# A layer normalisation's variance by a product with a matrix of ones and a Newton step, inside one inference step of a convolution trunk

## Chip, cores and metric

One core of a Trainium2 chip. The time is that of the whole program on the device, in microseconds (us); three runs of each kernel are compared by their median.

## What is computed

The program is one layer of a streaming encoder on 4096 prompt frames and 32 frames of a running stream, 1024 channels, all in fp32. Cut to what matters:

```python
def mixer_layer(x, hist_a, hist_b, norm_g, w_in, conv_a_w, conv_b_w, conv_b_bias, ln_b_g, ln_b_b, w_out):
    hn = rms_norm(x, norm_g)
    proj = jnp.einsum('btd,de->bte', hn, w_in.astype(hn.dtype))
    h_a, b_a, c_a, z_a, a_b, g_b, z_b = jnp.split(proj, SPLITS, axis=-1)
    conv_a, new_a = causal_dwconv(hist_a, c_a * h_a, conv_a_w)
    out_a = b_a * conv_a * jax.nn.silu(z_a)
    v_b = a_b * jax.nn.sigmoid(g_b)
    conv_b, new_b = causal_dwconv(hist_b, v_b, conv_b_w)
    s_b = jax.nn.silu(layer_norm(conv_b + conv_b_bias, ln_b_g, ln_b_b))
    out_b = s_b * jax.nn.silu(z_b)
    mixed = jnp.concatenate([out_a, out_b], axis=-1)
    y = jnp.einsum('bte,ed->btd', mixed, w_out.astype(mixed.dtype))
    return x + y, new_a, new_b
```

A second `rms_norm` follows. The change is in `layer_norm`, which takes mean and variance of each frame over the 512 channels of group B, and in the order of the work around it.

## The kernel before

Channels lie on the partitions and frames along the free dimension, so the sums of the layer normalisation run across partitions, and TensorE makes them. Every large product is a Strassen product: seven products P1, P5, P6, P2, P7, P3, P4 (in this order) of half-sized blocks, each as split products (high and low parts in fp32r, three matmuls for each piece of 128 rows; lines 2422 to 2424).

The program has two large parts. The input projection and both convolutions run first (VectorE makes the 31 taps of convolution B; line 2149). The output part, which the change touches most, follows. It runs over 16 pairs of row tiles, m = 0 to 15, 256 frames each, and over the seven products i = 0 to 6 of a pair. The layer normalisation works on blocks L of 512 frames, two pairs to a block; the work for block L is spread over the 14 products (slots 0 to 13) of pairs m = 2(L-1) and 2L-1, one block ahead of the pairs that use it. The last block, L = 8, is 128 wide. Block 0 is normalised in the late part of the projection.

There is no scheduler. Each engine runs a list written by hand, and semaphores order them. Inside the loop over (m, i), a table `LN_SLOT` (and `FIRST_LN_SLOT` for block 1) says in which slot each step of the normalisation is issued on each engine, and inside one slot the order is that of the code.

What has to be known of these lists for the steps below:

- GpSimd makes the channel sums of the next block in slot 12 (`sums`, lines 1309 and 1312), behind the low part of the next pair's P1 form (`form_low`, line 1352). ScalarE makes the high part of the sum (`sum_high`, line 1672), GpSimd the low part (line 1317), TensorE the mean (`mean`, lines 2530 and 2531) behind product 0.
- VectorE subtracts the mean (`centre`, line 2161), ScalarE squares, VectorE adds the squares (`square_sums`, lines 2166 and 2168).
- TensorE then sums the squares by `column_sums` (slot 5), with the squares as the weights and one column of ones moving, 128 frames at a time, so that frames come to lie on partitions. ScalarE scales (line 1677), GpSimd takes the power -0.5 (line 1323), and `column_spread` (slot 7) spreads the result over all partitions with an identity.
- VectorE multiplies by it (`normalise`, line 2175, slot 7), ScalarE applies SiLU (line 1684, slot 8), VectorE multiplies by the gate (`gate`, line 2189, slot 10).
- VectorE adds each product from PSUM into the rows (`add_product`, line 2340). P6 uses the bank of P1, P7 that of P6, P4 that of P7 and P3 that of P5, so each of these products waits for the addition before it. VectorE also scales finished rows (`finish_rows`, line 2347) and makes the sums and low parts of the next pair's forms (lines 2205 to 2226) in slots 5 and 6 of a pair.
- ScalarE makes the high parts of the forms (`form_high_of`, line 1648): P1 at i = 4, P5 and P6 at i = 5, each in program order behind whatever stands ahead of it.

Of the kernel before, what the change touches and what calls it, by code (L numbers as in the profile page):

```python
# [4 lines left out]
F32 = mybir.dt.float32  # L5
# [5 lines left out]
P = 128  # L11
# [231 lines left out]
def build_program(nc, A):  # L243
    ctx = ExitStack()
    with ctx:
# [35 lines left out]
        var_cols = sb("ln_var_columns", [P, RT])  # L281
        rstd_cols = sb("ln_rstd_columns", [P, RT])
# [247 lines left out]
        ln_cols_sum = sem("ln_columns_summed")  # L530
        ln_cols_var = sem("ln_columns_var")
        ln_cols_rstd = sem("ln_columns_rstd")
# [150 lines left out]
        def col_tiles(L):  # L683
            return 1 if is_last(L) else RT
# [58 lines left out]
        def h_part_of(m, i):  # L743
# [3 lines left out]
        FIRST_LN_SLOT = {"sums": 1, "sum_high": 3, "sum_low": 3, "mean": 4, "squares": 5, "square_sums": 6, "columns": 8,  # L747
                         "spread": 10, "silus": 11, "gate": 12}
        LN_SLOT = {"sums": -2, "sum_high": -2, "sum_low": -2, "mean": 1, "squares": 2, "square_sums": 3, "columns": 5,
                   "spread": 7, "silus": 8, "gate": 10}  # L750
# [13 lines left out]
        def _(sp):  # L764
# [187 lines left out]
            def first_loads(g, c):  # L952
# [12 lines left out]
                if g == 11 and c in (0, 2):  # L965
                    if c == 0:
# [3 lines left out]
                        sp.wait_ge(ln, ln_event(0, "squares"))  # L970
                    else:
                        sp.wait_ge(ln_cols_sum, 1)
# [4 lines left out]
                if g == 13 and c == 0:  # L977
                    sp.wait_ge(dve_made, DVE_AT[period_of("bz", 4, JT - 1), "z"])
                    sp.wait_ge(u_state, 16 * 8)
                    load_x_rows(0)  # L980
# [165 lines left out]
        def _(pool):  # L1146
# [154 lines left out]
            def sums(L):  # L1301
# [5 lines left out]
                else:  # L1307
                    pool.wait_ge(ln, ln_event(L - 1, "gated" if L == 1 else "squares"))
# [106 lines left out]
            for n in range(III, PERIODS):  # L1415
# [8 lines left out]
                for part in range(3):  # L1424
                    for r in late_split(n, part):
                        late_low(r)
                    if part == 0 and g == 10:
                        column_rstd(0)
# [5 lines left out]
            for m in range(PAIRS):  # L1434
                for i in range(7):
# [6 lines left out]
                    if ln_due(m, i, "columns"):  # L1442
                        column_rstd(ln_due(m, i, "columns"))
# [19 lines left out]
        def _(act):  # L1463
# [210 lines left out]
            def column_var(L):  # L1674
                c = col_tiles(L)
                act.wait_ge(ln_cols_sum, L + 1)
# [117 lines left out]
            for n in range(III, PERIODS):  # L1794
# [11 lines left out]
                if g == 10:  # L1806
                    column_var(0)
# [893 lines left out]
```

## Time and profile before

| | |
|---|---|
| median of 3 runs | 1511.53 us (1511.13 to 1513.31) |
| profiled execution, its own time | 1511.45 us |
| its span | 1509.7 us |
| TensorE (PE) busy | 1500.2 us, 99% |
| weight loads (PEld) busy | 1323.4 us, 88% |
| VectorE (DVE) busy | 1307.6 us, 87% |
| ScalarE (ACT) busy | 594.4 us, 39% |
| GpSimd (POOL) busy | 653.5 us, 43% |
| granted TensorE clock | 0.999 |

Shares are of the span, averaged over the program. In the listings a start time is counted from the start of the span, and a group shows its count, its busy time and the mean of one.

### The profile page before, as it was taken

Reading aid. Unit: us, or ns where it says so; the run is one execution under the profiler, and the core shown is the slowest. Engines: PE = TensorE matmul, PEld = TensorE weight load, DVE = VectorE, ACT = ScalarE, POOL = GpSimd, SP = SyncE. Lnnn points to the kernel's source line nnn. Section 1 sums busy time; section 2 is a strip of 40 time slices with the busy share of each in tenths; the row PEclk is TensorE's granted clock in tenths of the full one; section 3 lists DMA queues with packets and bytes.
Section 4 is the critical chain, followed back from the end, with each engine's and each line's share of the span. In section 5 each row is a group of like instructions: output and inputs, shape, how many; then the busy total and the mean of one; then the engine's idle time right before and its main releaser. Section 6 shows DMA issues by size and latency. Waiting matters only on the chain.

```text
span 1509.7 us, 19729 instructions
## 1 busy us (share of the span) xinstructions
PE 1500.2 (99%) x7114; PEld 1323.4 (88%) x7114; DVE 1307.6 (87%) x1333; ACT 594.4 (39%) x987; POOL 653.5 (43%) x568
## 2 busy tenths in 40 slices
PE   9999999999999999999999999999999999999998
PEld 8999999888888888888888888888888878888886
DVE  7899999999998898899899895798898798888876
ACT  7554432432342343333253322224343344444433
POOL 4887778311424232332532252116664544444441
PEclk9999999999999999999999999999999999999999
DMA  6797968688988889999889888766877755455541
GB/s 250 306 352 289 366 254 321 211 301 310 317 287 294 281 279 336 303 342 283 262 271 320 311 269 261 242 214 213 237 223 227 265 193 170 172 189 186 177 153 70
DMA packets 119512, 388.97 MB, mean 258 GB/s; under 512 B 17848, under 2 KB 23096, under 8 KB 115832
## 3 DMA queue, kind: packets, MB, share of 16 engines
q1 hardware_dynamic: 116872, 387.57, 75.5%
q8 instruction: 57, 0.93, 0.2%
q10 hardware_dynamic: 2544, 0.14, 0.1%
q14 instruction: 39, 0.32, 0.1%
HBM read 279.19 MB, written 108.47 MB: 257 GB/s over the span
## 4 chain that ended last, share of the span: by engine, by line
PE 98%; DVE 2%; issue 0%; ACT 0%; POOL 0%; POOLq 0%; DVEq 0%; ACTq 0%
PE ps L2422 32%; PE ps L2424 32%; PE ps L2423 32%; PE ps L2544 0%; PE ps L2537 0%; PE ps L2557 0%; DVE conv_b L2189 0%; DVE h_rows_odd L2347 0%; DVE w_ring L2212 0%; DVE ln_tmp_b L2166 0%; DVE w_ring_f L2161 0%; PE ps L2628 0%; PE ps L2531 0%; PE ps L2530 0%; DVE ps L2205 0%
## 5 line engine op out<-in xcount | busy, mean ns | idle before, releaser
L2149 DVE SCALAR_TENSOR_TENSOR ps<-v,conv_b_taps,ps 128x920 f32<-128x920 f32 (+2 forms) x580 | 630.8, 1088 | 17.3
L2422 PE MATMUL ps<-xf,w_ring 128*128 128x460 f32 (+1 forms) x1624 | 602.9, 371 | 0.3 <-issue 0.3
L2424 PE MATMUL ps<-xf,w_ring 128*128 128x460 f32 (+1 forms) x1624 | 602.6, 371 | 0.0
L2423 PE MATMUL ps<-xf,w_ring 128*128 128x460 f32 (+1 forms) x1624 | 600.8, 370 | 0.0
L2422 PEld LDWEIGHTS ps<-xf,w_ring 128*128 128x128 f32 x1624 | 305.4, 188 | 34.2 <-issue 1.2
L2423 PEld LDWEIGHTS ps<-xf,w_ring 128*128 128x128 f32 x1624 | 305.4, 188 | 34.0
L2424 PEld LDWEIGHTS ps<-xf,w_ring 128*128 128x128 f32 x1624 | 304.9, 188 | 34.2
L1605 ACT ACTIVATE sets<-ps 128x460 f32<-128x460 f32 x168 | 92.8, 553 | 475.9 <-PE ps L2424 475.9
L1346 POOL TENSOR_TENSOR w_ring<-w_ring_f,w_ring 128x512 fp32r<-128x512 f32 x28 | 38.9, 1388 | 215.3 <-ACT w_ring L1635 215.3
L1297 POOL TENSOR_TENSOR sets<-sets 128x460 f32<-128x460 f32 x42 | 56.5, 1346 | 129.1 <-ACT sets L1605 129.1
L1237 POOL TENSOR_TENSOR w_ring<-w_ring_f,w_ring 128x512 fp32r<-128x512 f32 x56 | 74.9, 1349 | 64.4 <-ACT w_ring L1539 64.0
L2422 PE MATMUL ps<-out_forms,w_ring 128*128 128x512 f32 x240 | 94.5, 394 | 0.3 <-DVE h_rows_even L2340 0.3
L2424 PE MATMUL ps<-out_forms,w_ring 128*128 128x512 f32 x240 | 93.5, 390 | 0.0
L2423 PE MATMUL ps<-out_forms,w_ring 128*128 128x512 f32 x240 | 93.5, 389 | 0.0
L2422 PE MATMUL ps<-xf 128*128 128x448 f32 (+1 forms) x224 | 83.3, 372 | 0.0
L2424 PE MATMUL ps<-xf 128*128 128x448 f32 (+1 forms) x224 | 82.6, 369 | 0.0
L2423 PE MATMUL ps<-xf 128*128 128x448 f32 (+1 forms) x224 | 82.3, 367 | 0.0
L1196 POOL TENSOR_TENSOR x_raw<-x_raw,rstd_spread 128x460 f32<-128x460 f32 x56 | 68.0, 1249 | 32.2 <-DMA rstd_spread<-rstd_spill 32.2
L2340 DVE TENSOR_TENSOR h_rows_odd<-ps,h_rows_odd 128x512 f32<-128x512 f32 x56 | 38.5, 687 | 30.5 <-PE ps L2424 30.5
L1539 ACT ACTIVATE w_ring<-w_ring_f 128x512 fp32r<-128x512 f32 x56 | 35.0, 631 | 72.3 <-DMA w_ring_f<-in_w_in 72.1
L2422 PEld LDWEIGHTS ps<-out_forms,w_ring 128*128 128x128 f32 x240 | 45.1, 188 | 10.2 <-issue 0.7
L2424 PEld LDWEIGHTS ps<-out_forms,w_ring 128*128 128x128 f32 x240 | 45.0, 188 | 9.7
(237 smaller groups left out, 2216.9 us busy)
## 6 DMA issues: line engine op xcount, KB each, us to landing
w_ring<-weight_forms SPq DMA_DIRECT2D x294, 512.0 KB, 5.4
weight_forms<-xf SPq DMA_DIRECT2D x7, 2048.0 KB, 12.6
weight_forms<-w_ring SPq DMA_DIRECT2D x7, 2048.0 KB, 11.4
x_row<-in_x_prompt SPq DMA_DIRECT2D x28, 512.0 KB, 7.4
out_weight_forms<-w_ring SPq DMA_DIRECT2D x28, 512.0 KB, 6.6
w_ring_f<-in_w_in SPq DMA_DIRECT2D x56, 256.0 KB, 3.5
x_raw<-in_xT SPq DMA_DIRECT2D x31, 460.0 KB, 6.9
xf_f<-in_w_in SPq DMA_DIRECT2D x24, 512.0 KB, 6.3
```

Source lines behind the costliest of these rows:

```text
L1196: pool.tensor_tensor(part, part, spread[:, 0:TB], ALU.mult).then_inc(x_scaled, 1)
L1237: pool.tensor_tensor(ring[:, slot, 1, :], ring_f32[:, slot, 1, :], ring[:, slot, 0, :].bitcast(F32), ALU.subtract).then_inc(late_lo, 1)
L1297: pool.tensor_tensor(sets[:, s, QC, :], sets[:, s, QC, :], sets[:, s, QD, :], ALU.add).then_inc(c22_made, 1)
L1346: pool.tensor_tensor(low, of, high, ALU.subtract).then_inc(wr_lo, 1)
L1539: act.activation(ring[:, slot, 0, :], ring_f32[:, slot, 1, :], ACT.Copy).then_inc(late_hi, 1)
L1605: act.activation(sets[:, n % 2, quarter, :], ps[:, bank, 0:TB], ACT.Copy).then_inc(copied, 1)
L2149: dve.scalar_tensor_tensor(dst, window, wb[:, j, k:k + 1], part, ALU.mult, ALU.add).then_inc(taps_done, 1)
L2340: dve.tensor_tensor(to, ps[:, bank_of_product(m, i), :], to, ALU.add).then_inc(h_add, 1)
L2422: pe.matmul(out, ahi, bhi, start=(start and x == 0), stop=False, skip_group_check=goes_on)
L2423: pe.matmul(out, ahi, blo, start=False, stop=False, skip_group_check=goes_on)
L2424: mm = pe.matmul(out, alo, bhi, start=False, stop=(stop and x == len(terms) - 1), skip_group_check=goes_on)
```

## The change

The variance is now a product of the sum of squares with the same matrix `mean_w` that the mean uses (1/512 everywhere). For that the sum of squares is split into a high part (ScalarE) and a low part (VectorE). The result stands in PSUM on all partitions at once. ScalarE makes a first value of the inverse root as exp(-0.5 ln(var + eps)), and VectorE refines it with one Newton step of three operations. The two column products, the scaling on ScalarE and the power on GpSimd are gone.

The slots of the later steps change: normalise from 7 to 10, SiLU from 8 to 10, gate from 10 to 12. VectorE's list changes too: for even m, the additions of the previous pair's P4 and of P1 go into `last_lows_of(m)`, ahead of the low parts of P7 and P3; for odd m both row scalings stand in slot 1.

```diff
-        LN_SLOT = {"sums": -2, "sum_high": -2, "sum_low": -2, "mean": 1, "squares": 2, "square_sums": 3, "columns": 5,
-                   "spread": 7, "silus": 8, "gate": 10}
+        LN_SLOT = {"sums": -2, "sum_high": -2, "sum_low": -2, "mean": 1, "squares": 2, "square_sums": 3, "square_sum_parts": 4,
+                   "variance": 5, "seed": 7, "rstd": 9, "normalise": 10, "silus": 10, "gate": 12}
...
-            def column_rstd(L):
-                c = col_tiles(L)
-                pool.wait_ge(ln_cols_var, L + 1)
-                pool.tensor_tensor(rstd_cols[:, 0:c], var_cols[:, 0:c], minus_half[:, :].to_broadcast([P, c]),
-                                   ALU.pow).then_inc(ln_cols_rstd, 1)
...
+            def square_sum_high(L):
+
+                w = ln_width(L)
+                act.wait_ge(ln, ln_event(L, "squares"))
+                act.activation(ta_split[:, 1, 0:w], tb[:, 0, 0:w], ACT.Copy).then_inc(ln_var_hi, 1)
+
+            def rstd_seed(L):
+
+                w = ln_width(L)
+                act.wait_ge(ln_var, L + 1)
+                act.activation(ln_rstd_places(L)[0], ps[:, STAT_BANK, 0:w], ACT.Ln,
+                               bias=ln_eps[:, :]).then_inc(ln_log, 1)
+                act.wait_ge(ln_log, L + 1)
+                act.activation(ln_rstd_places(L)[0], ln_rstd_places(L)[0], ACT.Exp, scale=-0.5).then_inc(ln_seed, 1)
...
+            def square_sum_low(L):
+
+                w = ln_width(L)
+                dve.wait_ge(ln_var_hi, L + 1)
+                dve.tensor_tensor(ta_split[:, 0, 0:w], tb[:, 0, 0:w], ta_split[:, 1, 0:w].bitcast(F32),
+                                  ALU.subtract).then_inc(ln_var_lo, 1)
+
+            def refine_rstd(L):
+
+                w, (y, t) = ln_width(L), ln_rstd_places(L)
+                dve.wait_ge(ln_seed, L + 1)
+                dve.scalar_tensor_tensor(t, y, -0.5, y, ALU.mult, ALU.mult).then_inc(ln_step, 1)
+                dve.wait_ge(ln_step, 3 * L + 1)
+                dve.scalar_tensor_tensor(t, ps[:, STAT_BANK, 0:w], ln_eps[:, :], t, ALU.add, ALU.mult).then_inc(ln_step, 1)
+                dve.wait_ge(ln_step, 3 * L + 2)
+                dve.scalar_tensor_tensor(y, t, 1.5, y, ALU.add, ALU.mult).then_inc(ln_step, 1)
...
@@ last_lows_of
-                if m == 2:
-                    add_product(1, P4)
-                    add_product(2, P1)
+                if m and m % 2 == 0:
+                    add_product(m - 1, P4)
+                    add_product(m, P1)
                 low_of(m, P7, 0)
                 low_of(m, P3, 1)
...
@@ VectorE's loop over (m, i)
-                    elif m and m != 2 and i in (1, 2):
+                    if m % 2 and i == 1:
+                        finish_rows(m - 1, 0)
+                        finish_rows(m - 1, 1)
+                    elif m % 2 == 0 and m > 2 and i in (1, 2):
                         finish_rows(m - 1, i - 1)
...
@@ TensorE
-            def column_sums(L):
-            def column_spread(L):
+            def variance(L):
+
+                w, dst = ln_width(L), ps[:, STAT_BANK, :]
+                pe.wait_ge(ln_var_lo, L + 1)
+                pe.matmul(dst[:, 0:w], mean_w[:, :], ta_split[:, 1, 0:w], start=True, stop=False)
+                pe.matmul(dst[:, 0:w], mean_w[:, :], ta_split[:, 0, 0:w], start=False, stop=True).then_inc(ln_var, 1)
```

**VectorE, an odd pair of the steady output part.** The first list is of before, from the row scaling and addition behind P4 of the even pair to the sums for the next pair; h_rows are the output rows, the 2048-wide operations are normalise (line 2175) and gate (line 2189).

```order
L2340 TENSOR_TENSOR h_rows_even<-ps,h_rows_even 128x512
L2175 TENSOR_TENSOR conv_b<-conv_b,ps 128x2048
L2340 TENSOR_TENSOR h_rows_odd<-ps,h_rows_odd 128x512
L2347 SCALAR_TENSOR_TENSOR h_rows_even<-h_rows_even,rstd,final_gain 128x1024
L2340 TENSOR_TENSOR h_rows_odd<-ps,h_rows_odd 128x512
L2347 SCALAR_TENSOR_TENSOR h_rows_even<-h_rows_even,rstd,final_gain 128x1024
L2340 TENSOR_TENSOR h_rows_odd<-ps,h_rows_odd 128x512
L2189 TENSOR_TENSOR conv_b<-conv_b,silu_zb 128x2048
L2340 TENSOR_TENSOR h_rows_odd<-ps,h_rows_odd 128x512 x2
L2205 TENSOR_TENSOR ps<-out_a,conv_b 128x512
```

Now the same stretch of the changed kernel, whose lines have other numbers (2367 is the addition, 2374 the row scaling, 2189 to 2193 the Newton step, 2200 normalise, 2214 gate).

```order
L2367 TENSOR_TENSOR h_rows_even<-ps,h_rows_even 128x512
L2367 TENSOR_TENSOR h_rows_odd<-ps,h_rows_odd 128x512
L2374 SCALAR_TENSOR_TENSOR h_rows_even<-h_rows_even,rstd,final_gain 128x1024 x2
L2367 TENSOR_TENSOR h_rows_odd<-ps,h_rows_odd 128x512
L2189 SCALAR_TENSOR_TENSOR ln_tmp_b<-ln_tmp_b 128x512
L2191 SCALAR_TENSOR_TENSOR ln_tmp_b<-ps,ln_eps,ln_tmp_b 128x512
L2193 SCALAR_TENSOR_TENSOR ln_tmp_b<-ln_tmp_b 128x512
L2367 TENSOR_TENSOR h_rows_odd<-ps,h_rows_odd 128x512
L2200 TENSOR_TENSOR conv_b<-conv_b,ln_tmp_b 128x2048
L2367 TENSOR_TENSOR h_rows_odd<-ps,h_rows_odd 128x512 x2
L2214 TENSOR_TENSOR conv_b<-conv_b,silu_zb 128x2048
```

Normalise has moved behind the additions of P1, P5 and P6 of the odd pair, both row scalings and the Newton step, and the gate now stands directly ahead of the sums for the next pair.

**ScalarE, the same place.** In the changed kernel 1679 and 1682 are the logarithm and the exponential, 1688 SiLU, 1643 a form's high part (`<-out_a` is P1's of the next pair, `<-ps` P5's and P6's) and 1667 the high part of the next block's channel sum.

```order
L1679 ACT_TABLE_LOAD
L1679 ACTIVATE ln_tmp_b<-ps,ln_eps 128x512
L1682 ACT_TABLE_LOAD
L1682 ACTIVATE ln_tmp_b<-ln_tmp_b 128x512
L1688 ACT_TABLE_LOAD
L1688 ACTIVATE conv_b<-conv_b,ln_b,ln_g 128x512 x4
L1643 ACTIVATE out_in_form<-out_a 128x512
L1667 ACTIVATE w_ring<-w_ring_f 128x512
L1643 ACTIVATE w_ring<-ps 128x512 x2
```

Before, this stretch begins with SiLU and is the same from there on; what is new are three table loads and two activations ahead of it, and that SiLU itself waits for the later normalise.

## Rows read from the trace of the kernel before

**Rows 1.** The page's busy times, and the chain that ended last

```profile
PE 1500.2 (99%) x7114; PEld 1323.4 (88%) x7114; DVE 1307.6 (87%) x1333; ACT 594.4 (39%) x987; POOL 653.5 (43%) x568
...
PE 98%; DVE 2%; issue 0%; ACT 0%; POOL 0%; POOLq 0%; DVEq 0%; ACTq 0%
```

**Rows 2.** Group by line and form: the column sums (busy, mean ns)

```profile
L2537 PE MATMUL ps<-ones,ln_tmp_b 128*128 128x1 f32 x66 | 8.0, 240 | 1.4 <-DVE ln_tmp_b L2168 1.4
```

**Rows 3.** Timeline of TensorE around mean and column products (start, duration)

```profile
1295.72 0.39 PE L2530 MATMUL ps<-w_ring,mean_w 128*128 128x512 f32 x1
...
1296.18 0.40 PE L2422 MATMUL ps<-out_forms,w_ring 128*128 128x512 f32 x1
...
1307.09 0.95 PE L2537 MATMUL ps<-ones,ln_tmp_b 128*128 128x1 f32 x8
...
1308.22 0.40 PE L2423 MATMUL ps<-out_form_p,w_ring 128*128 128x512 f32 x1
...
1313.56 1.05 PE L2544 MATMUL ps<-ident,ln_rstd_columns 128*128 128x128 f32 x8
...
1314.69 0.39 PE L2423 MATMUL ps<-out_forms,w_ring 128*128 128x512 f32 x1
```

**Rows 4.** The critical chain: two column sums one block apart

```profile
1266.59 0.79 PE ps L2537 x8
...
1307.25 0.79 PE ps L2537 x8
```

**Rows 5.** Timeline of VectorE, pairs 5 to 7 (a bracket gives idle time before)

```profile
1290.73 0.69 DVE L2212 TENSOR_TENSOR w_ring<-ps,w_ring 128x512 fp32r<-128x512 f32 x1 [0.72 <-ACT w_ring L1648]
...
1293.86 0.68 DVE L2212 TENSOR_TENSOR out_in_form<-ps,out_in_form 128x512 fp32r<-128x512 f32 x1
...
1295.92 0.69 DVE L2340 TENSOR_TENSOR h_rows_even<-ps,h_rows_even 128x512 f32<-128x512 f32 x1
1296.53 2.28 DVE L2161 TENSOR_TENSOR w_ring_f<-w_ring_f,ps 128x2048 f32<-128x2048 f32 x1
1298.72 1.42 DVE L2347 SCALAR_TENSOR_TENSOR h_rows_odd<-h_rows_odd,rstd,final_gain 128x1024 f32<-128x1024 f32 x1
...
1301.86 0.68 DVE L2340 TENSOR_TENSOR h_rows_even<-ps,h_rows_even 128x512 f32<-128x512 f32 x1
...
1304.20 0.69 DVE L2168 TENSOR_TENSOR ln_tmp_b<-ln_tmp_b 128x512 f32<-128x512 f32 x1
...
1307.29 0.69 DVE L2340 TENSOR_TENSOR h_rows_even<-ps,h_rows_even 128x512 f32<-128x512 f32 x1 [1.79 <-PE ps L2424]
...
1314.60 0.68 DVE L2340 TENSOR_TENSOR h_rows_even<-ps,h_rows_even 128x512 f32<-128x512 f32 x1
```

**Rows 6.** Timeline of ScalarE: SiLU and a form's high part, pair 5

```profile
1276.85 2.94 ACT L1684 ACTIVATE conv_b<-conv_b,ln_b,ln_g 128x512 f32<-128x512 f32 x4 [1.47 <-DVE conv_b L2175]
1279.69 0.62 ACT L1648 ACTIVATE w_ring<-out_a 128x512 fp32r<-128x512 f32 x1
```

**Rows 7.** Timeline of GpSimd: P1's low part, then the next block's sums

```profile
1280.38 2.13 POOL L1352 TENSOR_TENSOR w_ring<-out_a,w_ring 128x512 fp32r<-128x512 f32 x1 [2.69 <-ACT w_ring L1648]
1284.27 3.08 POOL L1309 TENSOR_TENSOR w_ring_f<-w_ring_f 128x1024 f32<-128x1024 f32 x1 [1.75 <-DMA w_ring_f<-conv_spill]
1287.43 1.29 POOL L1312 TENSOR_TENSOR w_ring_f<-w_ring_f 128x512 f32<-128x512 f32 x1
```

**Rows 8.** Timeline, end of pair 1: VectorE's gate, GpSimd's sums beside it

```profile
1204.34 4.24 DVE L2189 TENSOR_TENSOR conv_b<-conv_b,silu_zb 128x2048 f32<-128x2048 f32 x1
...
1204.03 2.40 POOL L1309 TENSOR_TENSOR w_ring_f<-w_ring_f 128x1024 f32<-128x1024 f32 x1 [4.47 <-DMA w_ring_f<-conv_spill]
1206.51 3.23 POOL L1312 TENSOR_TENSOR w_ring_f<-w_ring_f 128x512 f32<-128x512 f32 x1
```

**Rows 9.** Timeline of ScalarE in the projection: a table load and the activation behind it

```profile
1122.25 1.28 ACT L1589 ACT_TABLE_LOAD   x1
1123.54 0.56 ACT L1589 ACTIVATE sets<-ps 128x460 f32<-128x460 f32 x1
```

More of the change, by code:

```diff
@@ L745, in h_part_of @@
             return hrow[m % 2][:, row, DA * half:DA * (half + 1)]
-        FIRST_LN_SLOT = {"sums": 1, "sum_high": 3, "sum_low": 3, "mean": 4, "squares": 5, "square_sums": 6, "columns": 8,
-                         "spread": 10, "silus": 11, "gate": 12}
-        LN_SLOT = {"sums": -2, "sum_high": -2, "sum_low": -2, "mean": 1, "squares": 2, "square_sums": 3, "columns": 5,
-                   "spread": 7, "silus": 8, "gate": 10}
+        FIRST_LN_SLOT = {"sums": 1, "sum_high": 3, "sum_low": 3, "mean": 4, "squares": 5, "square_sums": 6,
+                         "square_sum_parts": 6, "variance": 8, "seed": 8, "rstd": 9,
+                         "normalise": 10, "silus": 10, "gate": 12}
+        LN_SLOT = {"sums": -2, "sum_high": -2, "sum_low": -2, "mean": 1, "squares": 2, "square_sums": 3, "square_sum_parts": 4,
+                   "variance": 5, "seed": 7, "rstd": 9, "normalise": 10, "silus": 10, "gate": 12}
         def ln_due(m, i, step):
@@ L2324, in _ @@
                     first_ln[n - III](0)
+                if n - III == 11:
+                    normalise(0)
                 if n - III == 12:
@@ L2380, in _ @@
                 for i in range(7):
-                    if i and (m, i) not in ((0, 1), (1, 6), (2, 1)):
+                    if i and (m, i) != (1, 6) and (m % 2 or i > 1):
                         add_product(m, i - 1)
-                    elif m and i == 0 and m != 2:
+                    elif m % 2 and i == 0:
                         add_product(m - 1, P4)
@@ L2402, in _ @@
                         square_sums(ln_due(m, i, "square_sums"))
+                    if m == 2 and i == 3:
+                        finish_rows(1, 0)
+                        finish_rows(1, 1)
+                    if ln_due(m, i, "square_sum_parts"):
+                        square_sum_low(ln_due(m, i, "square_sum_parts"))
                     if m + 1 < PAIRS and i == 6:
@@ L2531, in mean @@
                 pe.matmul(dst[:, 0:w], mean_w[:, :], ta_split[:, 0, 0:w], start=False, stop=True).then_inc(ln_mean, 1)
-            def column_sums(L):
-                pe.wait_ge(ln, ln_event(L, "squares"))
-                for c in range(col_tiles(L)):
-                    mm = pe.matmul(ps[:, STAT_BANK, c:c + 1], tb[:, 0, P * c:P * (c + 1)], ones[:, :],
-                                   start=True, stop=True)
-                mm.then_inc(ln_cols_sum, 1)
-            def column_spread(L):
-                pe.wait_ge(ln_cols_rstd, L + 1)
-                for c in range(col_tiles(L)):
-                    mm = pe.matmul(ps[:, STAT_BANK, P * c:P * (c + 1)], rstd_cols[:, c:c + 1].to_broadcast([P, P]),
-                                   ident[:, :], start=True, stop=True)
-                mm.then_inc(ln_var, 1)
+            def variance(L):
[3 more added lines that the diff above has]
+                pe.matmul(dst[:, 0:w], mean_w[:, :], ta_split[:, 0, 0:w], start=False, stop=True).then_inc(ln_var, 1)
             def first_mean_square(b):
@@ L2584, in _ @@
                     mean(0)
[L2585 to L2586 removed]
                 if n == III + 11:
[L2588 removed]
+                    variance(0)
                 late_tile(n, 0)
@@ L2639, in _ @@
                         mean(ln_due(m, i, "mean"))
-                    if ln_due(m, i, "columns"):
-                        column_sums(ln_due(m, i, "columns"))
-                    if ln_due(m, i, "spread"):
-                        column_spread(ln_due(m, i, "spread"))
+                    if ln_due(m, i, "variance"):
+                        variance(ln_due(m, i, "variance"))
                     out_product(m, i)
```

64 lines of the change are left out of this document (29 added, 35 removed).

## Prediction, made before the result was known

> **What bounds the kernel now.** I read the busy times first: TensorE is busy 99% of the span, VectorE 87%, the other two about 40% [rows 1]. The chain that ended last says the same, 98% of it is TensorE. So two things can move the time: work taken off TensorE, microsecond for microsecond, and waits put into it, where nothing is hidden. VectorE's 13% idle looks like cover, but it is an average; what counts is in which slot a result is needed. So I went to the timelines of one block of the output part, two pairs, which repeats every 40.66 us (1266.59 to 1307.25) [rows 4].
>
> **What TensorE is spared.** Column sums: from the start of the eight matmuls to the second matmul of the next product 1.13 us pass (1307.09 to 1308.22) where one step of 0.23 would, so the group costs 0.90; the spread costs the same (1313.56 to 1314.69) [rows 3]. Together 1.80 us a block. The new variance is the pair of matmuls that the mean is: 1295.72 to 1296.18, 0.46 us [rows 3]. So 1.34 us less for each of the eight full blocks, and for the last, narrow one (2 of the 66 records of a kind [rows 2]) an estimated 0.3: 11.0 us in all. TensorE alone would need 40.66 - 1.34 = 39.3 us a block, and one slot of it is (1307.09 - 1296.18)/4 = 2.73 us [rows 3].
>
> **What the other engines get.** For each full block VectorE gets one 512-wide subtraction (0.69) and three 512-wide operations of the Newton step; I price them at 0.73 with their hand-over, from the 512-wide rows of 0.69 (a 1024-wide operation of their kind took 1.42) [rows 5]. Bounds: 0.61, the step between two additions, and 0.73. That is 2.9 us. ScalarE gets a copy of 0.62, two activations of about that size and three table loads; a load took 1.28 and the activation behind it began 0.01 after its end (1122.25, 1123.54) [rows 9]. GpSimd loses one small power. As totals all this fits. The loads stand ahead of their waits in ScalarE's list, so SiLU's is hidden while ScalarE waits for normalise.
>
> **The walk through one block.** What decides is the order. Normalise, SiLU and gate move from slots 7, 8, 10 to 10, 10, 12, and behind SiLU in ScalarE's list stand the high part of the next pair's P1 form, then the high part of the next block's channel sum, then those of P5 and P6. GpSimd makes P1's low part and only then the channel sums. So a late SiLU holds a chain over ScalarE, GpSimd, ScalarE and VectorE. I follow it from the start of P1's addition in an even pair (time 0), with durations of before:
>
> - VectorE, even pair: addition and the two low parts 3 x 0.61, centre to row scaling 2.19, scaling to P6's addition 3.14 (1298.72 to 1301.86) [rows 5]: that addition starts at 7.2. Then it and the 1024-wide sum of squares: before 2.34 to the next start (1301.86 to 1304.20), with GpSimd's low part of P1 beside it, which now comes later; I take 0.6 + 1.2, the 1.2 being half of the 2048-wide 2.28. The second sum (0.69) ends at 9.7, ScalarE's copy at 10.4, VectorE's low part at 11.2. TensorE's variance starts at 11.3 with its weight load.
> - TensorE: 0.46 + 3 x 2.73 and 0.2 of pipeline: P1 of the odd pair is done at 20.1. VectorE is there before: P7's to P4's addition took 7.3 (1307.29 to 1314.60) [rows 5], from 11.1 to 18.4.
> - VectorE, odd pair: P1's addition to 20.7, both scalings 2.5 (3.14 less an addition) to 23.3, P5's addition to 23.9, Newton step to 26.1, P6's addition to 26.7, normalise 2.28 to 29.0. The first value for the step is ready at about 23.7 (half row square 1.5 after P4's addition, two loads, two activations): just in time.
> - ScalarE: SiLU, then 2.84 after its start P1's high part (1276.85 to 1279.69) [rows 6], at 31.8. GpSimd starts P1's low part 0.69 later (1280.38), takes 2.13, then 3.16 and 1.29 for the sums [rows 7]: 39.1. ScalarE's two high parts 1.2: 40.4.
> - VectorE: low part of P5 to that of P7 3.13 (1290.73 to 1293.86), one more addition 0.6 [rows 5], then P1's addition of the next even pair: 44.2.
>
> This is a closed loop of 44.2 us, over three engines that each wait for another, longer than TensorE's own 39.3. Before, the same loop did not close, as SiLU stood two slots earlier: the sums began at 1284.27, after a wait for a DMA, and P1's addition came in time at 1295.92 [rows 5, 7]. So each block costs 44.2 - 40.7 = 3.5 us more, with TensorE waiting 4.9 in it: for the mean, for P6's addition ahead of P7, and for the low part of the squares ahead of the variance.
>
> **The sum.** Six passages from a block to the next (blocks 1 to 7): 6 x 3.5 = 21. In block 2 the row scalings stand between the second sum of squares and its low part: 0.5. In the late projection (block 0) 1.3 is spared, but VectorE gets 2.9 us more there; I take 0. The last block gives 0.3 back. 1511.45 + 21 + 0.5 - 0.3 = 1532.7, say 1533 us. The profiled execution's own time, 1511.45, is that of the median, 1511.53, so nothing is shifted.
>
> **Bounds.** GpSimd's three operations are what I know least: 2.13 + 3.16 + 1.29 = 6.6. Alone a 512-wide one took 1.29 and the 1024-wide as little as 2.40 [rows 7, 8]: 1.6 less, with the Newton step at 0.61 2.0 less, times six: 1521. Beside the gate, the second one took 3.23 [rows 8]: 1.9 more, 1545. In this spot the changed kernel's gate runs beside them in every block. The Trainium skill, GPSIMD Engine Reference, Specifications, says that GpSimd's SBUF interface is shared with VectorE and contended by VectorE instructions with two SBUF inputs; the gate is one. By that rule, the trace agrees: the gate took 4.24 us beside them, where centre, of the same width, took 2.28 [rows 5, 8].
>
> **Rivals.**
> - *Faster (the other side).* The loop is shorter than I make it, so TensorE waits for nothing and all 11.0 us come out: 1500.5. It decides at a loop of 40.66; for that 3.5 us of my walk would have to be wrong in one place, GpSimd's three operations taking 3.1 and not 6.6. For it: VectorE's idle share is larger than what it gets. Against it: even at the lower bounds the loop is 42.2. Chance 0.09, and 0.04 for a draw near 1511.
> - *Slower, but with GpSimd at its low rows:* 1521 to 1526, chance 0.17.
> - *The likeliest:* loop of 43.3 to 45.3 us, 1526 to 1540, chance 0.48.
> - *Contention in every block,* up to 1547: chance 0.14.
> - *The first value is late.* If a switch of tables cost more than its load, the Newton step would wait. At 1.4 us more for each of two switches it starts 2.6 later than in my walk; seven times, 18 on top: 1551. The row of before speaks against it: the activation began 0.01 after the load [rows 9]. Chance 0.05. The same end is reached if one of TensorE's waits grows so long that the granted clock falls to 1.2 GHz; before it was 0.999 throughout, with waits up to 1.4 us [rows 2]. Chance 0.03. The Trainium skill, ScalarE: Activation LUTs, What ACT_TABLE_LOAD costs, is the page that says so: 1.28 us for the load and 1.38 for a drain, 2.66 for each switch; by it the time would be that of this rival.
>
> **How the numbers follow.** A measurement of this kernel tells 0.2% (3 us) from no change. Faster 0.09, same 0.04, slower 0.87. From 1518 to 1547 the range leaves out the faster case and most of the last rival, under 2 in 10.
>
> **What would show it.** Right: no columns' matmuls; TensorE idle about 4 to 5 us in each block from pair 2 on, with VectorE's addition (P6's) and its low part of the squares as the ones it waits for, and GpSimd's mean part; the even pairs' P1 additions some 44 us apart; ScalarE's P5 high part started by the high part of the channel sum behind GpSimd. Wrong: additions 39.3 to 40 us apart and TensorE without idle time, or ScalarE's exponential as the releaser of the Newton step. What would break the prediction is GpSimd's part of the loop, or a transfer (the next block's convolution rows, which came at 1284.27 before) that starts later and takes its place.

## The result, and the profile after

The changed kernel takes 1553.35 us (median; 1551.37 to 1556.71), the kernel before 1511.87 us in the same runs. The ratio is 1.0273, with an interval of 1.0263 to 1.0284: slower by 41.5 us. The forecast was 1533, range 1518 to 1547: the direction is right, the time lies 6 us above the range, and the loss is twice the 21.5 that I gave it. The profiled execution took 1552.25 us, span 1550.5.

The page's busy times of the changed kernel, against [rows 1]:

```profile
PE 1510.5 (97%) x7000; PEld 1320.6 (85%) x7000; DVE 1330.5 (86%) x1369; ACT 640.8 (41%) x1031; POOL 643.4 (41%) x559
```

TensorE has 114 matmuls fewer and is busy 10 us more: part of its work ran slower. What it waited for (total us, times, longest), which was 1.4 us for the column sums before [rows 2]:

```profile
PE ps L2564 <- POOL w_ring L1322: 18.8, 6, 3.2
PE ps L2456 <- DVE h_rows_odd L2367: 9.0, 7, 2.4
...
PE ps L2571 <- DVE w_ring L2182: 1.8, 2, 1.4
```

L2564 is the mean's matmul, L1322 GpSimd's low part of the channel sum. P1's additions in the even pairs, VectorE's timeline, give the length of each block; first the changed kernel:

```profile
1172.89 0.68 DVE L2367 TENSOR_TENSOR h_rows_even<-ps,h_rows_even 128x512 f32<-128x512 f32 x1
...
1221.28 0.68 DVE L2367 TENSOR_TENSOR h_rows_even<-ps,h_rows_even 128x512 f32<-128x512 f32 x1
...
1361.30 0.68 DVE L2367 TENSOR_TENSOR h_rows_even<-ps,h_rows_even 128x512 f32<-128x512 f32 x1
...
1408.70 0.68 DVE L2367 TENSOR_TENSOR h_rows_even<-ps,h_rows_even 128x512 f32<-128x512 f32 x1
...
1454.71 0.68 DVE L2367 TENSOR_TENSOR h_rows_even<-ps,h_rows_even 128x512 f32<-128x512 f32 x1
...
1498.87 0.68 DVE L2367 TENSOR_TENSOR h_rows_even<-ps,h_rows_even 128x512 f32<-128x512 f32 x1
```

Then the first two and the last of the kernel before:

```profile
1171.58 0.68 DVE L2340 TENSOR_TENSOR h_rows_even<-ps,h_rows_even 128x512 f32<-128x512 f32 x1
...
1215.01 0.68 DVE L2340 TENSOR_TENSOR h_rows_even<-ps,h_rows_even 128x512 f32<-128x512 f32 x1
...
1458.56 0.69 DVE L2340 TENSOR_TENSOR h_rows_even<-ps,h_rows_even 128x512 f32<-128x512 f32 x1 [0.28 <-PE ps L2424]
```

When the output part starts the changed kernel is 1.3 us late; one block later 6.3; at its seventh addition 36.8 (1454.71, and 1458.56 less one block of 40.66); at the eighth 40.3. So the loss grows with every passage, by 3.5 to 6.7 us, and there are seven passages.

One passage closely, with time 0 at 1267.76, as in the walk of the prediction. VectorE:

```profile
1267.76 0.68 DVE L2367 TENSOR_TENSOR h_rows_even<-ps,h_rows_even 128x512 f32<-128x512 f32 x1
...
1288.57 0.69 DVE L2367 TENSOR_TENSOR h_rows_odd<-ps,h_rows_odd 128x512 f32<-128x512 f32 x1 [0.79 <-PE ps L2458]
1289.62 3.51 DVE L2374 SCALAR_TENSOR_TENSOR h_rows_even<-h_rows_even,rstd,final_gain 128x1024 f32<-128x1024 f32 x2 [0.36 <-POOL rstd L1169]
...
1293.65 0.68 DVE L2189 SCALAR_TENSOR_TENSOR ln_tmp_b<-ln_tmp_b 128x512 f32<-128x512 f32 x1
...
1296.36 2.28 DVE L2200 TENSOR_TENSOR conv_b<-conv_b,ln_tmp_b 128x2048 f32<-128x2048 f32 x1
...
1310.48 0.69 DVE L2237 TENSOR_TENSOR w_ring<-ps,w_ring 128x512 fp32r<-128x512 f32 x1 [4.03 <-ACT w_ring L1643]
...
1314.21 0.68 DVE L2367 TENSOR_TENSOR h_rows_even<-ps,h_rows_even 128x512 f32<-128x512 f32 x1
```

ScalarE: the first value of the inverse root, SiLU, P1's high part, the channel sum's:

```profile
1288.56 1.28 ACT L1679 ACT_TABLE_LOAD   x1
1289.86 0.69 ACT L1679 ACTIVATE ln_tmp_b<-ps,ln_eps 128x512 f32<-128x512 f32 x1
1290.56 1.28 ACT L1682 ACT_TABLE_LOAD   x1
1291.86 0.63 ACT L1682 ACTIVATE ln_tmp_b<-ln_tmp_b 128x512 f32<-128x512 f32 x1
...
1298.68 2.93 ACT L1688 ACTIVATE conv_b<-conv_b,ln_b,ln_g 128x512 f32<-128x512 f32 x4 [4.89 <-DVE conv_b L2200]
1301.52 0.62 ACT L1643 ACTIVATE w_ring<-out_a 128x512 fp32r<-128x512 f32 x1
1309.34 0.63 ACT L1667 ACTIVATE w_ring<-w_ring_f 128x512 fp32r<-128x512 f32 x1 [7.20 <-POOL w_ring_f L1317]
```

GpSimd: P4's low part, P1's, the two channel sums, the sum's low part:

```profile
1289.56 1.30 POOL L1351 TENSOR_TENSOR w_ring<-w_ring_f,w_ring 128x512 fp32r<-128x512 f32 x1
1302.21 2.95 POOL L1351 TENSOR_TENSOR w_ring<-out_a,w_ring 128x512 fp32r<-128x512 f32 x1 [11.36 <-ACT w_ring L1643]
1305.13 2.84 POOL L1314 TENSOR_TENSOR w_ring_f<-w_ring_f 128x1024 f32<-128x1024 f32 x1
1308.05 1.26 POOL L1317 TENSOR_TENSOR w_ring_f<-w_ring_f 128x512 f32<-128x512 f32 x1
1310.04 1.27 POOL L1322 TENSOR_TENSOR w_ring<-w_ring_f,w_ring 128x512 fp32r<-128x512 f32 x1 [0.74 <-ACT w_ring L1667]
```

This is the forecast's loop, station by station, and 46.45 us long where I had 44.2: P1's high part starts at 33.8 (mine 31.8), GpSimd's sums end at 41.6 (39.1), the next addition is at 46.45 (44.2). VectorE waits 4.03 and ScalarE 7.20 for GpSimd, TensorE 3.15 for the mean:

```profile
1311.37 0.59 PE L2564 MATMUL ps<-w_ring,mean_w 128*128 128x512 f32 x1 [3.15 <-POOL w_ring L1322]
...
1313.24 0.76 PE L2456 MATMUL ps<-out_forms,w_ring 128*128 128x512 f32 x1 [0.86 <-DVE h_rows_odd L2367]
1313.81 0.63 PE L2457 MATMUL ps<-out_forms,w_ring 128*128 128x512 f32 x1
1314.23 0.63 PE L2458 MATMUL ps<-out_forms,w_ring 128*128 128x512 f32 x1
```

The second wait ends with the addition at 1312.42, which stands behind VectorE's low parts. Behind the first wait the matmuls step by 0.42 us, not 0.23 (1313.81 to 1314.23). The stretches of the trace (columns: length, busy time and count of PE, PEld, DVE, ACT, POOL, the granted clock, then share and GB/s of the DMA engines) say why: 0.50 is the lower level, 1.2 GHz. The stretch from 1268 lies behind the wait for the mean one block earlier.

```profile
1240.00:1260.00 20.00, 20.00 (x88) 16.27 (x88) 16.72 (x16) 10.51 (x16) 6.42 (x6) 1.00 0.65 214
1268.00:1270.00 2.00, 2.00 (x6) 1.52 (x6) 2.00 (x4) 1.79 (x5) 0.04 (x1) 0.50 0.00 0
1300.00:1311.00 11.00, 8.12 (x35) 6.00 (x33) 5.41 (x5) 3.80 (x8) 7.97 (x4) 1.00 0.61 191
1312.00:1316.00 4.00, 3.14 (x8) 2.21 (x8) 4.00 (x7) 3.48 (x9) 1.43 (x2) 0.50 0.00 0
```

### The profile page after: what moved, and what is told of

Its sections match the earlier page's. It is cut to its first block and busy times, and to the rows that moved or that the text cites. A ratio compares the mean times of both kernels' runs of the same rounds, so it can differ in the third digit from the quotient of the medians.

```text
span 1550.5 us, 19572 instructions
## 1 busy us (share of the span) xinstructions
PE 1510.5 (97%) x7000; PEld 1320.6 (85%) x7000; DVE 1330.5 (86%) x1369; ACT 640.8 (41%) x1031; POOL 643.4 (41%) x559
## 5 line engine op out<-in xcount | busy, mean ns | idle before, releaser
L2456 PE MATMUL ps<-out_forms,w_ring 128*128 128x512 f32 x240 | 99.4, 414 | 9.8 <-DVE h_rows_odd L2367 7.7
L2457 PE MATMUL ps<-out_forms,w_ring 128*128 128x512 f32 x240 | 97.5, 406 | 0.0
L2458 PE MATMUL ps<-out_forms,w_ring 128*128 128x512 f32 x240 | 97.0, 404 | 0.0
L2456 PEld LDWEIGHTS ps<-out_forms,w_ring 128*128 128x128 f32 x240 | 47.4, 197 | 25.8 <-DVE w_ring L2237 9.1
L1351 POOL TENSOR_TENSOR w_ring<-out_a,w_ring 128x512 fp32r<-128x512 f32 x11 | 22.6, 2052 | 88.6 <-ACT w_ring L1643 88.6
L2458 PEld LDWEIGHTS ps<-out_forms,w_ring 128*128 128x128 f32 x240 | 47.5, 198 | 10.7
```

The costliest lines, as they stand in the source:

```text
L1351: pool.tensor_tensor(form_part(m, i, 1), of, form_part(m, i, 0).bitcast(F32), ALU.subtract).then_inc(raw_lo, 1)
L2456: pe.matmul(out, ahi, bhi, start=(start and x == 0), stop=False, skip_group_check=goes_on)
L2457: pe.matmul(out, ahi, blo, start=False, stop=False, skip_group_check=goes_on)
L2458: mm = pe.matmul(out, alo, bhi, start=False, stop=(stop and x == len(terms) - 1), skip_group_check=goes_on)
```

## The experiments

Theory A: the slots close a loop through SiLU, P1's high part, GpSimd and the mean. The rivals: the new operations cost by themselves (B), or the granted clock does (C). All medians stand against 1511.9 to 1513.1 of the kernel before in the same runs. "Block" is the distance between the centre operations (VectorE, 128x2048, the mean subtracted) of the third and the seventh block, divided by four, from each run's own trace; it is 40.66 before and 46.74 in the changed kernel (1269.55 and 1456.50). It covers four of the seven passages, so two runs with the same block can still differ in their medians. "-Newton" leaves the Newton step out, so that the inverse root is the first value alone.

| Run | Edit | Median us | Ratio (interval) | Block us |
|---|---|---|---|---|
| e1 | before, with the new order alone | 1545.08 | 1.0215 (1.0198-1.0232) | 46.75 |
| e13 | e1, P1's high part ahead of SiLU | 1519.53 | 1.0046 (1.0031-1.0061) | 41.90 |
| e5 | changed, old order and slots | 1560.68 | 1.0317 (1.0299-1.0334) | 47.83 |
| e6 | e5 -Newton | 1532.24 | 1.0130 (1.0115-1.0145) | 43.82 |
| e7 | changed, old slots only | 1560.56 | 1.0317 (1.0301-1.0332) | 47.77 |
| e2 | changed -Newton | 1536.22 | 1.0160 (1.0145-1.0175) | 44.63 |
| e3 | changed, P1's high part ahead of SiLU | 1534.27 | 1.0146 (1.0131-1.0161) | 43.92 |
| e11 | e3 -Newton | 1517.08 | 1.0031 (1.0019-1.0042) | 41.25 |
| e4 | changed, TensorE kept busy in its wait | 1547.45 | 1.0234 (1.0219-1.0249) | 46.05 |
| e8 | changed, paired scalings behind normalise | 1546.96 | 1.0227 (1.0212-1.0242) | 45.75 |
| e10 | e8, first value earlier | 1534.58 | 1.0146 (1.0131-1.0161) | 43.82 |
| e9 | e10 and e3 | 1536.65 | 1.0160 (1.0145-1.0175) | 44.23 |
| e12 | e9, P4's low part ahead of rows' factor | 1531.36 | 1.0124 (1.0109-1.0139) | 43.63 |
| e14 | e12 -Newton | 1524.27 | 1.0076 (1.0059-1.0092) | 42.70 |
| e15 | changed, P4's low part ahead of rows' factor | 1542.27 | 1.0195 (1.0181-1.0209) | 45.71 |
| e16 | e15 and e3 | 1532.57 | 1.0135 (1.0121-1.0149) | 43.63 |
| e17 | e16 -Newton | 1523.82 | 1.0071 (1.0058-1.0085) | 43.07 |

**The order alone.** e1 gives the kernel before the slots 10, 10, 12 and VectorE's new order, with none of the new arithmetic:

```diff
-                   "spread": 7, "silus": 8, "gate": 10}
+                   "spread": 7, "normalise": 10, "silus": 10, "gate": 12}
```

> Variance by the column products as before, but normalise and SiLU in slot 10, gate in slot 12, and the additions and row scalings in the order of the changed kernel. Theory A (the closed loop through SiLU, P1's form, GpSimd's sums and P5's form sets the pace): slower than before although neither the Newton step nor the table loads are there; the loop lacks the Newton step (2.1 us) and the low part of the squares, so about 44 us instead of 46.5, near 1535 us (1528 to 1542). Theory B (the added work on VectorE and ScalarE is the cost): within 4 us of before, 1508 to 1516.

It loses 32 us, 3 over A's bound: the order closes the loop by itself, and the wait is the forecast's (L2533 is the mean's matmul there, L1317 its low part):

```profile
PE ps L2533 <- POOL w_ring L1317: 12.8, 6, 2.6
```

But its block is 46.75, as long as with the Newton step, where A had 44. VectorE stands there ahead of normalise, for TensorE's product P6:

```profile
1336.35 0.69 DVE L2340 TENSOR_TENSOR h_rows_odd<-ps,h_rows_odd 128x512 f32<-128x512 f32 x1 [1.64 <-PE ps L2427]
```

So with the old arithmetic this piece of the loop goes through TensorE's own products, and not through VectorE's queue as in my walk; P1's addition of the odd pair also comes 1.0 us later after that of the even pair than in the changed kernel (21.84 against 20.81). The median is 8 us lower than the changed kernel's; in the traces, 3.7 us of that lie between the centres of the first and second block (38.58 against 42.27; 36.70 before).

Which piece of the order? e3 (in the changed kernel) and e13 (in e1) take P1's high part from behind SiLU on ScalarE:

```diff
-                    if m + 1 < PAIRS and i == 4:
+                    if m + 1 < PAIRS and i == (3 if m % 2 else 4):
                         form_high_of(m + 1, P1)
```

> The changed kernel with one line moved: on ScalarE the high part of the next even pair's P1 form stands ahead of SiLU. Theory A: GpSimd can make P1's low part and the channel sums while SiLU runs; the loop is then closed by SiLU, gate and VectorE's sums, about 42.2 us, TensorE's wait for the mean is gone and with it the half clock: 1522 us (1516 to 1530). Theory B (VectorE's work): no more than 5 us less, 1548 to 1553.

> The kernel before's column products with the new order of slots, additions and scalings (1545.08), and P1's high part ahead of SiLU on ScalarE. Theory A (what the order alone costs is P1's high part behind a late SiLU, and behind it P1's low part, GpSimd's sums and the mean): TensorE's wait for the mean goes, 1510 to 1520. Theory B (the late gate, or the additions of P1 and P6 and the paired scalings on VectorE, hold it): 1530 to 1545.

e13 gives 25.6 of the 32 us back, as A had it, and no wait for the mean is left; of the 6.6 that stay, TensorE's waits for additions make up 6.2. e3 gives 19 of 41, between its two expectations: the mean is in time, and the block falls to 43.9, not to TensorE's 39.3. What TensorE waits for in e3 is an addition of VectorE that stands behind the gate, the sums and the low parts of the forms:

```profile
PE ps L2456 <- DVE h_rows_odd L2367: 16.8, 12, 2.9
```

So there is a second loop right under the first: normalise, SiLU, gate, VectorE's sums and low parts, additions, TensorE.

**The new operations.** e2 leaves out the Newton step, e11 does so on top of e3:

```diff
-                dve.wait_ge(ln_step, 3 * L + 3)
+                dve.wait_ge(ln_seed, L + 1)
```

> The changed kernel without the Newton step's three operations (the first value is used as it is, so a refinement of the inverse root is left out). Theory A: the three stand inside the loop, so it gets 2.1 us shorter in each of 7 passages, 1538 us (1535 to 1542). Theory C (TensorE's long wait and the half clock behind it are the cost, VectorE is cover): about 1550 to 1553.

> P1's high part ahead of SiLU, and the Newton step left out (the inverse root is the seed alone). Theory A (both pieces lie in series on the same loop, so their gains of 19 and 17 us add up): 1513 to 1521. Theory B (once P1's high part is ahead, VectorE's additions behind the gate and the sums close the loop, and that does not hold Newton): 1526 to 1534.

The step is worth 17.1 and 17.2 us, inside A's range in both. Its 2.1 us of work shorten the block by 2.1 in e2 and by 2.7 in e11, so it lies on both loops at full length; a further 2.2 and 1.4 us are gained ahead of the first block's centre, where block 0 has the step too. e5 and e7 put the new operations into the old slots, where A saw room for them (and SiLU of block 1 into slot 11, as before); e5 also gives VectorE its old order back, and e6 is e5 without the Newton step:

```diff
-                   "variance": 5, "seed": 7, "rstd": 9, "normalise": 10, "silus": 10, "gate": 12}
+                   "variance": 5, "seed": 6, "rstd": 7, "normalise": 7, "silus": 8, "gate": 10}
```

> All of the new arithmetic (variance by a product, Ln and Exp, the Newton step), but with the order of before: seed in slot 6, Newton and normalise in slot 7, SiLU in slot 8, gate in slot 10, and VectorE's additions and row scalings where they stood. Theory A (the loss is the order: SiLU some 8 to 11 us late closes the loop through the mean): TensorE keeps the 11 us that it is spared and waits little, 1500 to 1510, faster than before. Theory B (VectorE's added 3.3 us a block and the table loads cost by themselves): 1518 to 1530.

> As the run before it, with the Newton step left out too, so the inverse root is the seed alone (the computation is changed in that). Theory A: with the old order Newton's 2.1 us lie in slack, so this is within 3 us of the run with it: 1499 to 1507. Theory B: 10 to 17 us below it, as in the new order, where leaving it out gave 17.

> The changed kernel with the slots of normalise, SiLU and gate moved back (7, 8, 10) and the Newton step in slot 7, but VectorE's additions of P1 and P6 and the paired row scalings left where the change put them. Theory A (the late slots are the loss): 1500 to 1513. Theory C (the moved additions and scalings cost by themselves, since the addition of P4 now stands where P1's stood and the two scalings stand together): 1525 or more.

A failed here: with the Newton step the old order is the slower one, with VectorE's additions in either place (so C's cause is not borne out by e7, though its time is). Without the step it is the other way round: e6 takes 1532.24 us, e2 1536.22. ScalarE's timeline in e5 shows it, between two sums of squares:

```profile
1330.76 1.28 ACT L1679 ACT_TABLE_LOAD   x1
1332.06 0.69 ACT L1679 ACTIVATE ln_tmp_b<-ps,ln_eps 128x512 f32<-128x512 f32 x1
1332.76 1.28 ACT L1682 ACT_TABLE_LOAD   x1
1334.06 0.63 ACT L1682 ACTIVATE ln_tmp_b<-ln_tmp_b 128x512 f32<-128x512 f32 x1
...
1335.73 1.06 ACT L1643 ACTIVATE out_in_form<-ps 128x512 fp32r<-128x512 f32 x2
```

and VectorE's:

```profile
1336.34 1.29 DVE L2237 TENSOR_TENSOR out_in_form<-ps,out_in_form 128x512 fp32r<-128x512 f32 x2 [3.44 <-ACT out_in_form L1643]
...
1340.37 3.23 DVE L2200 TENSOR_TENSOR w_ring_f<-w_ring_f,ln_tmp_b 128x2048 f32<-128x2048 f32 x1
1343.53 0.68 DVE L2367 TENSOR_TENSOR h_rows_odd<-ps,h_rows_odd 128x512 f32<-128x512 f32 x1
```

Leaving the Newton step out gives 28 us here, 4.0 a block, more than either theory had: 2.1 is the step, and 0.95 is normalise, which takes 2.28 in e6, where it no longer runs beside GpSimd. In slot 6 the 3.9 us of loads and activations stand ahead of the high parts of the next pair, for which VectorE waits 3.44; then Newton and a normalise of 3.23 stand ahead of the addition that TensorE needs, which waits up to 6.1 us for it (41.3 in all). So the late slots spare e5's stall and buy the first loop for it; neither order holds this arithmetic at the old speed. The B of that expectation was too low as well (1518 to 1530).

**The clock.** e4 gives TensorE twelve idle matmuls, into the bank that the mean overwrites, while it waits:

```diff
+                    for _ in range(12):
+                        pe.matmul(dst[:, :], mean_w[:, :], wf[:, P1, 0, 0, :], start=True, stop=True)
                 pe.wait_ge(ln_sum_lo, L + 1)
```

> The changed kernel with 12 idle matmuls (512 wide, about 0.23 us each, 2.8 us) into the statistics bank before TensorE waits for the mean, so that it does not stand still in its longest wait. If the granted clock stays at 1, P1's product of the odd pair comes 0.7 us earlier in each loop: about 1549 us (1545 to 1552). Theory C (the half clock is most of what my walk missed, 2.2 us a block): 1538 us.

The granted clock stays at its upper level, 2.4 GHz, and 5.9 us come back, inside the first range, under 1 us a passage:

```profile
1314.00:1318.00 4.00, 3.77 (x17) 3.15 (x18) 4.00 (x7) 2.80 (x7) 1.91 (x4) 1.00 0.02 4
```

The lower level behind the wait is a real cost, but a small one; theory C falls.

**Pieces of the loop, moved one by one.** e8 moves the two scalings behind normalise; e10 also puts the logarithm and exponential at the end of slot 6, ahead of the sums of squares, and the Newton step and normalise one slot earlier, each ahead of one more addition; e9 is e10 with P1's high part first. (In e10's text "the run before it" is e9; in e14's, further down, "the first run" is e12.)

```diff
-                    if m % 2 and i == 1:
+                    if m % 2 and i == 3:
                         finish_rows(m - 1, 0)
                         finish_rows(m - 1, 1)
```

The further lines of e10, at the end of ScalarE's slot:

```diff
-                   "variance": 5, "seed": 7, "rstd": 9, "normalise": 10, "silus": 10, "gate": 12}
+                   "variance": 5, "seed": 6, "rstd": 8, "normalise": 9, "silus": 10, "gate": 12}
...
+                    if ln_due(m, i, "seed") and i == 6:
+                        rstd_seed(ln_due(m, i, "seed"))
```

> The changed kernel with one edit: the two row scalings of the even pair stand behind normalise (ahead of the gate) instead of ahead of the Newton step. Theory A (the loop from P1's addition to the next mean holds the scalings' 3.5 us and the wait for their factor, 0.4): every one of seven passages gives back 3 to 4 us, 1524 to 1534. Theory B (VectorE only trades places, the gate and the sums behind it become late, or the scalings now stretch P1's low part on GpSimd): 1542 to 1553.

> As the run before it, but with P1's high part left behind SiLU. It stands against the run that moved only the scalings (1547), in which Newton then waited for Exp. Theory A (Exp on ScalarE is the piece that took the scalings' place; it now ends 1.6 to 2.4 us earlier in each of seven passages): 1531 to 1541. Theory B (something else on VectorE or GpSimd holds the loop there): 1543 to 1550.

> The changed kernel with three moves: P1's high part ahead of SiLU on ScalarE; the even pair's two row scalings behind normalise; and the seed (Ln, Exp) at the end of slot 6, straight behind the high parts of the next pair and ahead of the two sums of squares and P4's high part, with Newton in slot 8 and normalise in slot 9. Theory A (the loop is a series of pieces, and each of the three, once the one ahead of it is gone, gives back its own length: 19 us for the first, and a further 3 us a passage for scalings and seed together): 1504 to 1520. Theory B (with P1's high part out of the way the loop is closed elsewhere, by the additions queued behind VectorE's sums and low parts): 1526 to 1536.

e8 gives 6.4 us where A had 19 to 29: instead of the scalings VectorE now waited 2.03 us for TensorE's product P5 and 0.56 for the exponential, so 1.3 us a passage was all that was to be had, and P1's low part on GpSimd grew from 2.95 to 3.36 beside the scalings. e10 gives 12.4 us more, inside A's range; the exponential is earlier there and the Newton step no longer stands behind P5's addition, and the two were not tried apart. TensorE still waits for the mean in e10 (10.1 us in all), and GpSimd's sums wait for a load:

```profile
1298.39 2.49 POOL L1314 TENSOR_TENSOR w_ring_f<-w_ring_f 128x1024 f32<-128x1024 f32 x1 [2.75 <-DMA w_ring_f<-conv_spill]
```

e9 ends 0.7 us above B's range. With the exponential ahead of the sums of squares, GpSimd makes the rows' factor 4.0 us later after the centre than in e3 (22.9 against 18.9), and behind that P4's low part, which takes 3.17 beside normalise; for it the load of the next block's convolution rows waits, 5.9 later than in e3. SP's queue in e9, then GpSimd's timeline:

```profile
1293.56 0.38 SPq L1006 DMA_DIRECT2D w_ring_f<-conv_spill  x1
```

```profile
1290.37 3.17 POOL L1351 TENSOR_TENSOR w_ring<-w_ring_f,w_ring 128x512 fp32r<-128x512 f32 x1
...
1300.10 2.40 POOL L1314 TENSOR_TENSOR w_ring_f<-w_ring_f 128x1024 f32<-128x1024 f32 x1 [4.33 <-DMA w_ring_f<-conv_spill]
```

e12 puts P4's low part ahead of the rows' factor, and the logarithm right behind P4's high part; e14 leaves the Newton step out of it.

> As the three moves together (1536.65), but the seed now stands behind P4's high part (still ahead of the two sums of squares), and on GpSimd P4's low part of the odd pair stands ahead of the rows' factor. In the three moves' trace the conv load waited for that low part (issued at 1293.56, where the run with P1's high part alone had 1285.87) and GpSimd's sums waited for the load. Theory A (this load closed the loop): the load goes out about 8 us earlier relative to P1's addition, GpSimd's sums no longer wait for it, and the loop comes to 40 to 42 us: 1508 to 1522. Theory B (it only took the place of an equally late piece): 1526 to 1537.

> The first run of this call with the Newton step left out (the inverse root is the seed alone). Theory A (with 2.1 us less the loop falls under TensorE's own 39.3 us a block, and TensorE keeps what it is spared): 1500 to 1509, faster than the kernel before. Theory B (other pieces of the loop hold it over 41 us): 1512 to 1520.

The load goes out at 1284.92, 8.4 us earlier after the centre than in e9, as expected, and nobody waits for it any more, but only 5.3 us come back. That is B's range; e14 (1524.27) lies above both of its own: GpSimd's sums now run beside VectorE's scalings, and those take 5.04 us:

```profile
1293.04 5.04 DVE L2378 SCALAR_TENSOR_TENSOR h_rows_even<-h_rows_even,rstd,final_gain 128x1024 f32<-128x1024 f32 x2
```

**Contention by itself.** e15 is the changed kernel with P4's low part of the odd pairs ahead of the rows' factor on GpSimd; VectorE, ScalarE and TensorE do the same in the same order. e16 adds e3, e17 also leaves the Newton step out.

```diff
+                    if m % 2 and i == 0:
+                        form_low(m, P4)
                     if m and i == 0:
                         row_rstd(m - 1)
```

> The changed kernel with one edit on GpSimd: the odd pair's low part of P4 stands ahead of the rows' factor, so that it no longer runs beside VectorE's two row scalings (which took 3.5 us beside it, 2.5 in my sum). Theory A (VectorE and GpSimd slow each other when both read SBUF, and the loop holds the difference): the scalings take 2.5 us again, Newton starts about 0.9 us earlier in each of seven passages: 1545 to 1549. Theory B (the scalings' 3.5 has another reason, or Exp, ready at the same time, holds Newton anyway): 1551 to 1555.

> P1's high part ahead of SiLU (1534.27 alone) and P4's low part ahead of the rows' factor. Theory A: the same 0.9 us a passage, 1526 to 1530. Theory B: 1532 to 1536.

> P1's high part ahead of SiLU without the Newton step (1517.08; the inverse root is the seed alone), and P4's low part ahead of the rows' factor. Its block of 40.9 us is 1.6 over TensorE's own work. Theory A (the scalings' stretching is in that loop): 1509 to 1513, level with the kernel before or just under it. Theory B (VectorE's additions now wait for TensorE, so nothing more is to be had from VectorE): 1515 to 1519.

In e15 the two scalings take what the forecast gave them:

```profile
1287.29 2.48 DVE L2376 SCALAR_TENSOR_TENSOR h_rows_even<-h_rows_even,rstd,final_gain 128x1024 f32<-128x1024 f32 x2 [0.40 <-POOL rstd L1169]
```

2.48 us, not 3.51, in every passage, and the block is 1.03 shorter: contention was a term of the loop. That the two figures agree to the last digit is chance, since single blocks of one trace differ by over 1 us (45.05 to 46.28 in e15); from the first centre to the last the seven passages are 6.6 us shorter, 0.94 each. The median fell by 11 us, below A's range. The first 2.2 us of the difference between the traces are there before the first block's centre (1178.61 against 1180.81), where no edited operation stands; the other runs with the Newton step are at 1179.1 to 1181.6 there.

e16 gained only 1.7 (B's range), and e17 lost 6.7 to e11, outside both of its ranges: the earlier load lets GpSimd's sums run beside normalise, and both engines pay. e17, VectorE and GpSimd:

```profile
1284.41 4.33 DVE L2197 TENSOR_TENSOR conv_b<-conv_b,ln_tmp_b 128x2048 f32<-128x2048 f32 x1
```

```profile
1286.67 3.22 POOL L1317 TENSOR_TENSOR w_ring_f<-w_ring_f 128x512 f32<-128x512 f32 x1
```

Alone these take 2.28 and 1.26. The times read as if the two engines took turns: GpSimd's first sum runs from 1284.19 to 1286.58, normalise ends 2.16 us behind that, and the second sum ends 1.15 us behind normalise. No run tests this reading.

No version tried beats the kernel before; the nearest, e11, is 0.31% slower and lacks the Newton step.

## Why the forecast was half of the loss

Two terms of the sum failed, the length of the loop (44.2 us, measured 46.0 to 47.4) and the number of passages (six, measured seven).

- *The mechanism* ("a closed loop over three engines that each wait for another") was right, and so was most of the waiting: 29.6 us in the three rows above, 4.2 a passage, against the 4.9 forecast. The wait for the low part of the squares came twice only, 1.8 us in all. One named wait was another: not P6's addition ahead of P7 in the even pair, but an addition of the odd pair, queued behind VectorE's sums and low parts.
- *The number of passages* was wrong. "Six passages" times 3.5 left out the last one, to the narrow block, where I only counted what TensorE is spared (0.3). It cost 3.5 us.
- *The length of the loop* was mis-sized: 44.2, measured 46.0 to 47.4 in the steady passages. Six passages cost 35.5 us (36.8 less the 1.3 at the start), not 21: 2.4 more each. In the passage above I had the odd pair's P1 addition 0.7 too early (20.1, measured 20.8; behind the lower clock), no wait for the rows' factor (0.36), the scalings at 2.5 (3.51), and P1's low part at 2.13 (2.95); the sums were 0.35 shorter than my price. Together 2.5. Of these e15 shows the scalings' stretching as a cause and e4 the clock; the others are read from rows.
- *Contention* was priced for GpSimd alone, as a bound ("what I know least"), and in the wrong place: the changed kernel's gate ran beside P1's low part (2.95), and was over before the channel sums, which took 2.84 and 1.26. I took VectorE's own scalings at their undisturbed length, though the gate's 4.24 us stood in [rows 8]. The Trainium skill, GPSIMD Engine Reference, Specifications, names VectorE instructions with two SBUF inputs as what contends; the trace agrees for the scalings (3.51 against 2.48 in e15) and for normalise, whose factor now lies in SBUF (4.33 in e17 against 2.28 in the changed kernel).
- *Block 0* taken as 0: 1.3 in this trace, 0.7 by its centre (1180.81 against 1180.10), and between -1.5 and +1.5 in the other runs with the Newton step (-1.6 to -0.9 in the five without it). The step holds within scatter.
- *The late first value* did not happen: each activation began 0.01 to 0.02 us after its 1.28 us load, as [rows 9] had it, and the exponential (1292.49) was done before Newton's turn (1293.65). The 2.66 us that the Trainium skill, ScalarE: Activation LUTs, What ACT_TABLE_LOAD costs, gives for a switch are not seen. But the loads matter as length in ScalarE's queue: what stands ahead of the high parts in e5 is 3.9 us long, of which 2.56 are loads.
- *The clock* was put at 0.03 as a rival of its own end. It fell to 0.50 with the waits for the mean, and e4 prices it at about 6 us: the mechanism came, its price was that of a term.

The sum again: 1.3 + 35.5 + 3.5 + 0.5 for the rest is the 40.8 us between the spans. That the second loop (normalise to additions) holds e3, e12 and e16 at 43.6 to 43.9 is read from their waits, none of which is for the mean; which single operation would open it was not tried. e10 comes to 43.8 on the first loop, with the load in it. Nor does any run show TensorE's own 39.3 us a block: the shortest with the new variance is 41.25.

## What to carry to other kernels

Time taken off the bounding engine is worth nothing until every chain around it is shorter than its new block: walk the loop through all engines, count every passage, the last and narrow one too, and then look for the next loop that is longer than the block, behind the first. Price each operation in its new neighbourhood: the same pair of scalings took 2.5, 3.5 or 5.0 us, depending on what GpSimd did beside it. A move that frees a transfer or an engine earlier also moves its work next to something else, and may lose there what it gains (e12, e16, e17).

## What the runs showed of the hardware

- Behind a wait of 3.15 us for the mean, TensorE's granted clock was 0.50 (1.2 GHz) in the following stretch (1312 to 1316) and its matmuls stepped by 0.42 instead of 0.23 us; with idle matmuls in the wait (e4) it was 1.00 behind it (1314 to 1318). In e1 a wait of 2.06 us had the same effect (0.50 from 1354 to 1358).
- VectorE and GpSimd stretch each other: a GpSimd 512-wide operation from 1.26 to 3.22 (e17), VectorE's normalise from 2.28 to 4.33 (e17), its two scalings from 2.48 (e15) to 5.04 (e12). VectorE's additions, with one of their two operands in PSUM, kept their 0.69 us beside GpSimd's sum (e3, 1294.15 and 1295.22).
- A logarithm, an exponential and a SiLU in turn cost three table loads of 1.28 us a block; where nothing else held it, an activation followed its load within 0.02 us.
